# The step size moved into the exponents of the SSM preparation, one product per head for y, and D times x shared by ScalarE and VectorE

## The reference, cut to what matters

```python
dt = softplus(c_dt.reshape(b, t, 2, SSM_HEADS) + ssm_dt_bias)
da = dt * (-exp(ssm_a_log))
y_f, ss_f = ssd_scan(c_x * dt[:, :, 0, :, None], da[:, :, 0], c_b, c_c, s0[:, 0])
y_b, ss_b = ssd_scan(rev(c_x * dt[:, :, 1, :, None]), rev(da[:, :, 1]), rev(c_b), rev(c_c), s0[:, 1])
y = y_f + rev(y_b) + ssm_d[:, None] * c_x
# inside ssd_scan, within a chunk:
lmat = exp(where(lower, acum_l - acum_s, -inf))
y_diag = einsum('bclgn,bcsgn,bcgrls,bcsgrp', cc, bc, lmat, xc)
```

## Time and profile before

| | us |
|---|---|
| median of 3 runs (lowest, highest) | 3855.45 (3854.82, 3856.01) |
| the profiled execution, own time | 3851.78 |
| its span | 3850.1 |
| PE busy | 3656.9 (95%) |
| DVE busy | 2040.8 (53%) |
| ACT busy | 1088.9 (28%) |
| POOL busy | 639.8 (17%) |

### The profile page before, as it was taken

One profiled execution on the slowest core, in us unless ns is written; L12 is line 12 of the kernel. 1 busy time (PEld: TensorE's weight loads), 2 busy tenths in 40 slices (PEclk: granted clock), 3 DMA queues, 4 the chain that ended last, 5 costly groups with the idle time before them and its releaser, 6 DMA issues.

```text
span 3850.1 us, 68479 instructions
## 1 busy us (share of the span) xinstructions
PE 3656.9 (95%) x29057; PEld 3442.9 (89%) x29057; DVE 2040.8 (53%) x2522; ACT 1088.9 (28%) x1952; POOL 639.8 (17%) x698
## 2 busy tenths in 40 slices
PE   7999999999899899899989999999998998899998
PEld 5999999999888776899989999999997886588998
DVE  5531454233478776585375224523325877856743
ACT  3211121122345462332122111112224456342311
POOL 1110111122400234100011111112233003510000
PEclk8999999999899999999999999999998999999999
DMA  6332223233621387752333232323336114776422
GB/s 242 110 106 92 87 87 92 84 126 111 250 60 35 121 284 258 244 162 88 103 105 109 87 109 87 93 87 103 115 122 222 51 41 166 259 252 188 139 91 93
DMA packets 361201, 506.51 MB, mean 132 GB/s; under 512 B 82528, under 2 KB 284872, under 8 KB 357968
## 3 DMA queue, kind: packets, MB, share of 16 engines
q1 hardware_dynamic: 309880, 375.22, 29.9%
q0 software_dynamic: 35040, 103.09, 8.8%
q10 hardware_dynamic: 16000, 24.12, 1.9%
HBM read 330.62 MB, written 171.73 MB: 130 GB/s over the span
## 4 chain that ended last, share of the span: by engine, by line
PE 70%; DVE 9%; issue 9%; DMA 3%; SPq 3%; DVEq 3%; ACT 2%; POOL 1%; ACTq 0%; POOLq 0%
PE PSUM L828 10%; PE PSUM L829 10%; PE PSUM L830 10%; PE PSUM L1356 4%; PE PSUM L1358 4%; PE PSUM L1357 4%; PE PSUM L1635 4%; PE PSUM L1470 3%; PE PSUM L1457 2%; PE PSUM L1767 2%; PE PSUM L1769 2%; PE PSUM L1768 2%; PE PSUM L1436 1%; PE PSUM L1437 1%; SPq L690 1%
## 5 line engine op out<-in xcount | busy, mean ns | idle before, releaser
L828 PE MATMUL PSUM<-h_hi,w_hi 128*128 128x384 f32 x2304 | 772.0, 335 | 4.4 <-ACT conv_in L1941 1.8
L830 PE MATMUL PSUM<-h_hi,w_lo 128*128 128x384 f32 x2304 | 770.5, 334 | 0.0
L829 PE MATMUL PSUM<-h_lo,w_hi 128*128 128x384 f32 x2304 | 770.3, 334 | 0.0
L828 PEld LDWEIGHTS PSUM<-h_hi,w_hi 128*128 128x128 f32 x2304 | 433.1, 188 | 9.2 <-issue 9.1
L829 PEld LDWEIGHTS PSUM<-h_lo,w_hi 128*128 128x128 f32 x2304 | 433.0, 188 | 0.0
L830 PEld LDWEIGHTS PSUM<-h_hi,w_lo 128*128 128x128 f32 x2304 | 433.0, 188 | 0.0
L2323 POOL DMA_DIRECT2D proj_d<-leave x140 | 132.1, 944 | 1377.8 <-DVE leave L2654 540.0
L1356 PE MATMUL PSUM<-h_hi,w_hi 128*128 128x384 f32 x960 | 325.1, 339 | 0.0
L1357 PE MATMUL PSUM<-h_lo,w_hi 128*128 128x384 f32 x960 | 321.2, 335 | 0.0
L1358 PE MATMUL PSUM<-h_hi,w_lo 128*128 128x384 f32 x960 | 321.2, 335 | 0.0
L2760 DVE TENSOR_REDUCE row_max<-PSUM 128x1 f32<-128x1152 f32 x128 | 173.5, 1355 | 96.4 <-PE PSUM L1437 96.2
(11 more groups left out here) (404 smaller groups left out, 7326.5 us busy)
## 6 DMA issues: line engine op xcount, KB each, us to landing
proj_d<-leave POOLq DMA_DIRECT2D x140, 512.0 KB, 3.9
w_raw<-in_w_in SPq DMA_DIRECT2D x54, 1024.0 KB, 5.5
gdn_tile_d<-g_out SPq DMA_DIRECT2D x18, 1536.0 KB, 7.4
wide_br<-proj_d SPq DMA_DIRECT2D x48, 576.0 KB, 4.6
xs<-ssm_tok_d SPq DMA_DIRECT2D x32, 640.0 KB, 5.8
ssm_tok_d<-x_rest SPq DMA_DIRECT2D x36, 512.0 KB, 3.5
w_in<-in_w_in SPq DMA_DIRECT2D x16, 1024.0 KB, 6.3
av_t<-gdn_tile_d SPq DMA_DIRECT2D x28, 512.0 KB, 5.6
```

What stands on the lines that cost most here:

```text
L828: pe.matmul(dst, wh, x_hi[:, k, lo:hi], start=(k == 0), stop=False)
L829: pe.matmul(dst, wh, x_lo[:, k, lo:hi], start=False, stop=False)
L830: last = pe.matmul(dst, wl, x_hi[:, k, lo:hi], start=False, stop=(k == kt - 1))
```

## The change

The step size dt goes into the exponent: dt exp(a) = exp(a + ln dt). ln dt is made beside the other decays, split in a high and a low part (`step_hl`), transposed and stored like them (`steprow_d`), and loaded into rows 64 to 96 of `s_col`, where `head_of` has entries for it. As x is then the same for both directions, DVE adds the two exponentials and multiplies the sum by C B once, and PE makes one product per head, with xt itself. The x_dt tiles go. Halves are now outside and directions inside, in the exponents and the exponentials. D times x is made by ACT for heads 0 to 7 and by DVE for heads 8 to 15. xt0 takes the place of the second w_ssm.

```diff
 # projection, D_TERMS and D_SUMS on DVE and ACT
                         dve.tensor_copy(dt_[:].rearrange("p t d h -> p t (d h)"), D["soft"][:, :, 16:48])
+                        dve.tensor_scalar(D["neg"][:, :, 16:48], D["soft"][:, :, 16:48], 1e-37, None, ALU.max)
...
+                    if run == D_SUMS:
+                        act.wait_ge(decay_term, l * 3 + 2)
+                        act.activation(dec["u"][:, :, 16:48], dec["neg"][:, :, 16:48], ACT.Ln)
+                        act.drain()
+                        act.activation(dec["poly"][:, :, 16:48], dec["u"][:, :, 16:48], ACT.Exp, scale=-1.0).then_inc(decay_exp, 1)
...
+                        dve.wait_ge(decay_exp, l * 3 + 2)
+                        steps = D["poly"][:, :, 16:48]
+                        dve.tensor_tensor(steps, D["neg"][:, :, 16:48], steps, ALU.mult)
+                        dve.drain()
+                        dve.scalar_tensor_tensor(steps, steps, -1.0, D["u"][:, :, 16:48], ALU.add, ALU.add)
...
 # D_LAST on PE, ACT and SP
-                        pe.transpose(bank(6, P)[0:64], ssm_cols[:, 4 * P:4 * P + 64], ident).then_inc(decay_prod, 1)
+                        pe.transpose(bank(6, P)[0:64], ssm_cols[:, 4 * P:4 * P + 64], ident)
+                        for c in range(3):
+                            pe.transpose(bank(6, P, (c + 1) * P), step_cols[:, c * P:c * P + P], ident)
+                        pe.transpose(bank(7, P), step_cols[:, 3 * P:4 * P], ident)
+                        pe.transpose(bank(7, P, P)[0:64], step_cols[:, 4 * P:4 * P + 64], ident).then_inc(decay_prod, 1)
...
+                        act.activation(step_rows[:, 0:3], bank(6, 3 * P, P).rearrange("p (c n) -> p c n", n=P), ACT.Copy)
+                        act.activation(step_rows[:, 3], bank(7, P), ACT.Copy)
+                        act.activation(step_rows[0:64, 4], bank(7, P, P)[0:64], ACT.Copy).then_inc(row_made, 1)
...
+                sp.dma_start(flat_steps[0:512]...).then_inc(row_out, 16)
+                sp.dma_start(flat_steps[512:576]...).then_inc(row_out, 16)
 # SSM preparation, PE
-                    pe.wait_ge(sp_w, n * 4 + 2 + 2 * half)
+                    pe.wait_ge(sp_w, n * 2 + 1 + half)
                     for h in range(8 * half, 8 * half + 8):
-                        for d in range(2):
-                            for part in HALVES:
-                                last = pe.matmul(dst, w_ssm[d][:, h, part], x_dt[p][d][:, h], start=d == 0, stop=d == 1)
+                        for part in HALVES:
+                            last = pe.matmul(PSUM[part, h * SP_:(h + 1) * SP_], w_ssm[:, h, part], xt[p][:, h * SP_:(h + 1) * SP_], start=True, stop=True)
...
-                def exponents(t, d):
+                def exponents(t, half):
-                    for half in range(2):
-                        if t or d:
-                            pe.wait_ge(sp_e, n * 4 + 2 * d + half - 1)
+                    for d in range(2):
+                        if t or half:
+                            pe.wait_ge(sp_e, n * 4 + 2 * half + d - 1)
...
-                    if t == 1:
-                        pe.wait_ge(sp_w, n * 4 - 3)
 # ACT
-                    act.wait_ge(sp_cb, n * 2 + 1)
                     act.activation(xt[p][:, 0:512], PSUM[:, 0:512], ACT.Copy).then_inc(out_ready, 1)
...
-                        for h in ((0, 1, 2, 3, 4, 5), range(6, SH))[d]:
+                        for h in (range(0, 4), range(4, 8))[half]:
 # POOL
+                for at in (64, 80):
+                    pool.drain()
+                    pool.tensor_tensor(head_of[:], head_of[:], ident[:, at:at + SH], ALU.subtract)
...
+                    pool.dma_start(s_col[d][64:96], steprow_d[t, d]).then_inc(s_in[d], 16)
...
-                        pool.wait_ge(sp_d, (l * NT + t) * 4 - 2 + 2 * d)
+                        pool.wait_ge(sp_d, (l * NT + t) * 4 - 1 + d)
 # DVE
-                    times_dt(t, 0).then_inc(sp_cb, 1)
...
-                    dve.wait_ge(out_ready, n * 2 + 1)
-                    times_dt(t, 1)
-                    dve.drain()
                     dve.wait_ge(sp_dx, n)
                     for half in range(2):
+                        hs = slice(8 * half, 8 * half + 8)
+                        for d in range(2):
+                            dve.wait_ge(sp_e, n * 4 + 2 * half + d + 1)
+                            if d == 0:
+                                dve.sem_inc(waits_held, 1)
+                        dve.tensor_tensor(e_ssm[0][:, hs], e_ssm[0][:, hs], e_ssm[1][:, hs], ALU.add)
                         if t:
                             y_sum(t - 1, half)
-                        hs = slice(8 * half, 8 * half + 8)
-                        for d in range(2):
-                            dve.wait_ge(sp_e, n * 4 + 2 * d + half + 1)
-                            dve.tensor_tensor(w_ssm[d][:, hs], e_ssm[d][:, hs], again(cb[p][:, half], 8), ALU.mult).then_inc(sp_w, 1)
+                        dve.drain()
+                        dve.tensor_tensor(w_ssm[:, hs], e_ssm[0][:, hs], again(cb[p][:, half], 8), ALU.mult).then_inc(sp_w, 1)
                         if half == (0 if t else 1):
...
+                            dve.tensor_tensor(d_x[p][:, 8:SH], xt[p][:, 8 * SP_:D_MODEL]..., over(rows[:, 88:96], SP_), ALU.mult)
                             dve.tensor_tensor(x_rest[p][0][:], xt[p][:, 0:D_MODEL]..., over(dt_rest[:, 0, t], SP_), ALU.mult).then_inc(sp_xr, 1)
```

More of the change, by code:

```diff
@@ L278, in backbone_kernel @@
         xin = [place(a, f"xin{n}", [P, 12, P]) for n in range(2)]
-        xt = [place(a, f"xt{n}", [P, 1280]) for n in range(2)]
+        a[1] += 5120
+        xt = [None, place(a, "xt1", [P, 1280])]
         e_ssm = [place(a, f"e_ssm{d}", [P, SH, P]) for d in range(2)]
-        w_ssm = [place(a, f"w_ssm{d}", [P, SH, P]) for d in range(2)]
-        a2 = fresh([a[1], 0, ACTV[2]])
+        w_ssm = place(a, "w_ssm", [P, SH, P])
+        xt[0] = place(a, "xt0", [P, 1280])
+        a2 = fresh([ACTV[0] + 55296, 0, ACTV[2]])
         s_row = [place(a2, f"s_row{d}", [P, SH, P], F32R) for d in range(2)]
@@ L287, in backbone_kernel @@
         cb = [place(a2, f"cb{n}", [P, SG, P]) for n in range(2)]
-        x_dt = [[place(a2, f"x_dt0{d}", [P, SH, SP_]) for d in range(2)]]
+        a2[1] += 8192
         d_x = [None, place(a2, "d_x1", [P, SH, SP_])]
@@ L292, in backbone_kernel @@
         a2 = [WT[0] + 36864, WT[0] + 36864, WT[2]]
-        x_dt.append([place(a2, f"x_dt1{d}", [P, SH, SP_]) for d in range(2)])
+        a2[1] += 8192
         d_x[0] = place(a2, "d_x0", [P, SH, SP_])
@@ L2334, in _ @@
                     base += 2 * pairs
[L2335 removed]
+                pool.wait_ge(row_out, l * 112 + 112)
                 pool.sem_inc(waits_held, 1)
@@ L2631, in decay_values @@
                             dve.tensor_tensor(ssm_hl[:, :, d, 1], cum[:, d, :, 4:20], ssm_hl[:, :, d, 0].bitcast(F32), ALU.subtract)
+                        dve.wait_ge(decay_exp, l * 3 + 2)
[4 more added lines that the diff above has]
+                        dve.drain()
+                        for d in range(2):
+                            dve.tensor_copy(step_hl[:, :, d, 0], steps[:, :, 16 * d:16 * d + 16])
+                        dve.drain()
+                        for d in range(2):
+                            dve.tensor_tensor(step_hl[:, :, d, 1], steps[:, :, 16 * d:16 * d + 16], step_hl[:, :, d, 0].bitcast(F32), ALU.subtract)
                         dve.tensor_tensor(rest[:], tot[:], cum[:], ALU.subtract).then_inc(decay_term, 1)
                     elif run == D_LAST:
-                        dve.wait_ge(decay_exp, l * 2 + 2)
+                        dve.wait_ge(decay_exp, l * 3 + 3)
                         for d in range(2):
@@ L2874, in y_sum @@
                     dve.tensor_tensor(y_acc[:, t, cols_], PSUM[:, cols_], d_x[t % 2][:].rearrange("p h q -> p (h q)")[:, cols_], ALU.add).then_inc(sp_yd, 1)
-                def times_dt(t, half):
-                    hs = slice(8 * half, 8 * half + 8)
-                    for d in range(2):
-                        last = dve.tensor_tensor(x_dt[t % 2][d][:, hs], PSUM[:, 512 * half:512 * half + 512].rearrange("p (h q) -> p h q", q=SP_), over(dt_[:, t, d, hs], SP_), ALU.mult)
-                    return last
                 for t in range(NT):
@@ L2906, in _ @@
                                 dve.wait_ge(xy_stored, l * 160 + 160)
+                            dve.tensor_tensor(d_x[p][:, 8:SH], xt[p][:, 8 * SP_:D_MODEL].rearrange("p (h q) -> p h q", q=SP_), over(rows[:, 88:96], SP_), ALU.mult)
                             dve.tensor_tensor(x_rest[p][0][:], xt[p][:, 0:D_MODEL].rearrange("p (h q) -> p h q", q=SP_), over(dt_rest[:, 0, t], SP_), ALU.mult).then_inc(sp_xr, 1)
```

52 lines of the change are left out of this document (30 added, 22 removed).

## The result

| | before | changed |
|---|---|---|
| median of 4 runs (lowest, highest) | 3855.14 (3853.04, 3856.01) | 3882.19 (3877.87, 3894.33) |
| median in a second series (29 and 5 runs) | 3856.49 (3850.27, 3866.04) | 3878.49 (3875.49, 3880.47) |
| ratio, 95% interval | | 1.0067 [1.0052, 1.0082]; second series 1.0051 [1.0038, 1.0064] |
| profiled execution, own time; span | 3851.78; 3850.1 | 3877.87; 3876.2 |

Forecast were 3870, range 3853 to 3880, slower at 0.65. The direction was right; the time lies 2 us beyond the range (the second series lies inside it), and the growth is 1.5 to 1.8 times the +14.8.

What follows compares the result with a forecast made beforehand. A loop of waits through PE, ACT and DVE, not load, bounds the preparation's tiles. Layer 1 +11.6, layer 0 +1.5, projection +1.7 make +14.8 on 3855.45: 3870, own range 3862 to 3880, stated 3853 to 3880.

Steps and rivals of the forecast that it cites:

- Period of the loop: SSM preparation: one tile's loop of waits through PE, ACT and DVE takes 11.65 us, 0.19 more than now, at held clock.
- PE's idle time: SSM preparation, per tile: PE has nothing to do for 3.7 us in layer 1, some 2.2 in layer 0.
- rival (d): Preparation: removed products ran beside others, y's halves stay at 2.04, PE idles 2.7; 3872; chance 0.58 together with the forecast.
- The projection +1.7: Projection, two layers: five more transposes (0.55 a layer) and one more DVE tensor_scalar (0.3 a layer) add 1.7 us.
- Table loads: Projection: Ln, Exp and two loads of function tables fall into ACT's idle 12.57 us and cost nothing.
- clock, six periods of layer 1: Preparation, layer 1: PE's idle time drops its clock to 1.2 GHz in each tile, 1.9 us each.
- clock, layer 0: Preparation, layer 0: 2.2 us idle is at the edge, so a quarter of 2.4 us over five periods, +3.0.
- loop longer, both layers: Preparation: DVE's longer row of work adds 0.19 us to each of six periods in layer 1 and five in layer 0.
- first two tiles of layer 1: Preparation, layer 1: x_dt leaving the path could gain 0.85, which the low clock takes; counted 0.
- tails: End of the preparation: layer 1 gains 2.0, of which the low clock takes back 1.0; layer 0 gains 2.5.
- The one gap of 2.24 that had held: Kernel before, preparation: after 2.24 us idle PE's clock held, the ten transposes taking 1.31; it fell after 2.78 and 4.34.
- the unseen forms: DVE's in-place sum and D times x, shown in no row; each bounded 0.1 either way, period 11.4 to 11.9.

Runs made afterwards that it cites:

- e1_filled: Changed kernel with 14 extra unused matmuls per tile in layer 1 and 8 in layer 0, where PE waits for y_sum; 3864.85, ratio 1.0021.
- e3_half_y: Kernel before with one of the two directions of y left out on PE; 3856.67 against 3856.49, ratio 0.9997.
- e9_no_ln: Kernel before with only the projection's edits, their result unread, and an exponential in place of Ln; 3861.84 against 3857.55, ratio 1.0006.
- e7_before_again: Kernel before, unchanged, profiled a second time; that execution took 3857.63.
- e16_before_third: Kernel before, unchanged, profiled a third time; that execution took 3860.65.
- e8_rows_last: Kernel before with only the projection's edits, their result unread, and the new DRAM array declared last; 3858.44 against 3857.55, ratio 1.0006.
- e14_before_shifted: Kernel before with only the new DRAM array declared in its place and one 32 KB store to it; 3856.40 against 3855.70, ratio 1.0001.
- e17_before_rest_later: Kernel before with DVE's x_rest of direction 0 moved behind y_sum(t-1,1); 3866.95 against 3852.66, ratio 1.0033.
- e5_dx_act: Changed kernel with D times x for all 16 heads on ACT, none on DVE; 3870.08, ratio 1.0039.
- e13_changed_rows_last: Changed kernel with the new DRAM array declared last; 3877.92, ratio 1.0047 to the kernel before.
- e15_best_rows_last: Changed kernel with y_sums ahead, x_rest of direction 1 on DVE, second decay-row set for layer 0, new array last; 3851.52 against 3855.70, ratio 0.9989.

## Why the prediction was right in its direction and wrong in its size

**Right.** Period of the loop: 11.65 forecast, 11.80 measured with the clock held. PE's idle time: 3.7 and 3.73 in layer 1, 2.2 and 2.14 to 2.22 in layer 0. That it costs the clock, and that the clock then costs more than all the saved work brings: e1_filled shows it by putting work back, e3_half_y by taking work from the kernel before. Products of y at a good half of their time (1.15 for 32 where 64 took 2.04; rival (d) is out). The projection +1.7, measured +1.6. Table loads: in ACT's idle time, and e9_no_ln without them gained nothing that can be told.

**The stage as a whole** was +13.1 (11.6 and 1.5) by the forecast and is +13.2 by the profiles, but by luck: its terms were off and offset each other.

| term | forecast | measured |
|---|---|---|
| clock, six periods of layer 1 | +11.4 | +7.6 (78.4 against 70.8 filled) |
| clock, layer 0 | +3.0 | +5.5 (77.0 against 71.5 filled) |
| loop longer, both layers | +2.1 | +4.2 |
| first two tiles of layer 1 | 0 | +2.2 (24.9 to 27.1) |
| first two tiles of layer 0, first transposes | 0 | -1.4 |
| tails | -3.5 | -3.3 and -1.7 |

Layer 0 was mis-sized most: I gave the clock a quarter of its full price where 2.2 us idle stands at the edge, and it fell in four tiles of six. The one gap of 2.24 that had held was too little to go by, and the length of a gap doesn't decide alone. In e7_before_again, the same instructions as the kernel before, PE idled for 3.77 us at that same place and the ten transposes still ran at full speed:

```profile
1344.14 1.31 PE L1561 MATMUL PSUM<-cst,xin 128*128 128x128 f32 x10 [3.77 <-DMA xin<-proj_d]
```

In e16_before_third, again the same instructions, they took 2.40 behind 3.24 us there. In layer 1 I took it that every tile pays 1.9; each pays 1.3 on the mean. Before two of the seven the ten transposes took 1.28 and 1.30 and not 2.3, so where in the tile the clock is low differs, and with it the price.

**The step that failed** is the total: "11.6 + 1.5 + 1.7 = +14.8", read as the difference of the medians, with a range of the unseen forms and the clock in one stage. Everything outside was taken at nothing and at no scatter. The two stages that I summed did come out at +14.8 by the profiles. Between the profiles 22.5 us differ, 8 of them outside those stages, nearly all in the scans. How far that belongs to the change is open. The medians (+22, +22 and +27) say that some 7 to 12 us more than the stage sum are real. In eleven of the twelve series of kernels with the projection's edits the median is 2 to 9.5 us further above that of the kernel before than its own projection and preparation give (against the mean of the three profiles of the kernel before); the twelfth, e8_rows_last, is level, and the mean is 5. In the three kernels without the edits (e3_half_y, e14_before_shifted, e17_before_rest_later) this surplus is -0.2, -0.8 and 4.3. So some 4 us seem to go with the edits on the mean, and no run shows by what: each suspect taken away alone left a time that can't be told from the others, and the scans of kernels without the edits range over 10 us. The profiled execution that I started from (3851.78) was a good one: later ones of the same kernel took 3857.63 and 3860.65, and medians of it 3852.7 to 3857.5. With the three runs shown agreeing within 1.2 us I took the scatter for that small.

## What to carry to other kernels

Before work is taken from TensorE, whose granted clock can fall behind idle time, write down its idle time per period afterwards: cutting 2 us of products that lie beside the critical loop turned 1.3 us of idle time into 3.7 and made tiles of 11.5 us last 12.4 to 14.1. If the loop can't be shortened as well, keep filler work (here 13.6 us less by it) or don't cut. When work goes, the order has to be made anew: with the two y_sums moved ahead, the same arithmetic went from 13 to 9.9 us a tile in layer 1. And a sum over stages predicts the stages; for the median add what the untouched stages scatter, from more than one profile.

## What the runs showed of the hardware

- The idle time before a fall of the clock, in the changed kernel: behind 2.14 to 2.22 us it fell in four of six tiles of layer 0, behind 3.65 to 3.73 in six of seven of layer 1, in layer 1 of e5_dx_act behind 2.85 to 3.06 in all seven; yet sometimes only after the ten transposes had run at full speed (3290.03 in e3_half_y), and not behind 3.77 in e7_before_again. Layer 1's tiles repeated to 0.1 us in a second profile of the same kernel, and not in e13_changed_rows_last.
- DVE's operation with two operands in SBUF was held up beside x_rest on GpSimd: 1.22 became 2.77 and 3.40 us, so 1.9 us of work put on GpSimd cost DVE 1.5 to 2.2, more than the 1.13 of doing it on DVE.
- A load of 16 KB that GpSimd issues landed after 3.2 us in the median of the kernel before, and after 5.6 in the median, up to 7.7, in layer 0 of e15_best_rows_last with its shorter tiles.
- PE stood still for 1 to 2.3 us with no wait that the profile shows, inside or at the start of a run of like matmuls, in 22 of 38 GDN scans.
